# Two fused blocks on one core: the recurrent gates run among the other projections, the convolution's inputs are multiplied on their way out of the banks, and two output chunks are opened in free score banks

## What is computed

```python
u = rms_norm(h, mix_norm[l])
q, k, v, sc_b, sc_c, sc_x, lru_x, lru_g = jnp.split(u @ w_in[l], IN_SPLIT_POINTS, axis=-1)
y_da = diff_attention(q, k, v, ...)                   # 4 heads, two softmaxes each, then a norm per head
y_sc = sc_b * causal_dwconv(sc_c * sc_x, sc_conv_w[l])          # width 256
xr = causal_dwconv(lru_x, lru_conv_w[l]) + lru_conv_b[l]        # width 256
y_lru = jax.nn.gelu(lru_g) * rg_lru(xr, lru_wa[l], ...)         # two gates, then a scan over the tokens
h = h + jnp.concatenate([y_da, y_sc, y_lru], axis=-1) @ w_out[l]
x = h + 0.5 * swiglu(rms_norm(h, ffn2_norm[l]), ...)
```

## Time and profile before

| what | value |
|---|---|
| median of 3 runs | 3335.58 us |
| the profiled execution, its own time | 3334.97 us |
| its span, first to last instruction | 3333.0 us |
| TensorE busy | 3183.0 us, 96% |
| VectorE busy | 1540.9 us, 46% |
| ScalarE busy | 716.5 us, 21% |
| GpSimd busy | 1975.6 us, 59% |
| mean granted TensorE clock | 0.979 |

### The profile page before, as it was taken

The page is one execution under the profiler, slowest core; times in us unless marked ns, Lnnn a source line. Parts: engine busy times, 40 slices in busy tenths (PEclk is TensorE's granted clock), DMA queues, the critical chain, the costliest instruction groups (busy, mean ns, idle before and its releaser), DMA issues.

```text
span 3333.0 us, 44944 instructions
## 1 busy us (share of the span) xinstructions
PE 3183.0 (96%) x15410; PEld 2618.1 (79%) x15410; DVE 1540.9 (46%) x1978; ACT 716.5 (21%) x1454; POOL 1975.6 (59%) x1566
## 2 busy tenths in 40 slices
PE   8998999989989999699998989999999997999998
PEld 7777888877778888588887678888888886788886
DVE  6577322275772322644227564431444247564422
ACT  3353110044531100411112221110111012321110
POOL 6324766653237666377666357776677665277763
PEclk9999999999999999899999999999999998999999
DMA  4111322221113222122222112223222232122221
GB/s 168 52 39 51 107 97 98 95 90 51 39 51 107 94 95 98 54 94 94 101 98 101 58 64 94 95 95 101 91 99 94 97 109 83 39 89 99 96 95 64
DMA packets 82023, 286.47 MB, mean 86 GB/s; under 512 B 9531, under 2 KB 13020, under 8 KB 81628
## 3 DMA queue, kind: packets, MB, share of 16 engines
q1 hardware_dynamic: 76032, 275.81, 24.6%
q10 hardware_dynamic: 5852, 8.78, 0.8%
HBM read 280.89 MB, written 3.67 MB: 85 GB/s over the span
## 4 chain that ended last, share of the span: by engine, by line
PE 89%; DVE 6%; issue 2%; ACT 1%; POOL 1%; DMA 0%; DVEq 0%; SPq 0%; ACTq 0%; POOLq 0%
PE bank_v L452 19%; PE bank_v L454 18%; PE bank_v L453 18%; PE bank_a L452 8%; PE bank_a L453 8%; PE bank_a L454 8%; PE bank_v L667 1%; PE bank_a L646 1%; PE bank_s L800 1%; PE bank_v L815 1%; PE bank_s L685 1%; DVE mix L1948 1%; PE bank_a L491 0%; DVE lru_x L1931 0%; PE bank_s L803 0%
## 5 line engine op out<-in xcount | busy, mean ns | idle before, releaser
L426 POOL TENSOR_TENSOR w_lo<-raw,w_hi 128x1024 fp32r<-128x1024 f32 x520 | 1321.4, 2541 | 41.6
L423 POOL TENSOR_TENSOR zero<-zero 128x1 f32<-128x1 f32 x520 | 132.3, 255 | 1280.0 <-PE bank_v L454 967.0
L452 PE MATMUL bank_v<-xn_hi,w_hi 128*128 128x512 f32 (+1 forms) x1648 | 633.9, 385 | 41.2 <-DVE da_v L2001 31.7
L453 PE MATMUL bank_v<-xn_lo,w_hi 128*128 128x512 f32 (+1 forms) x1648 | 624.5, 379 | 0.0
L454 PE MATMUL bank_v<-xn_hi,w_lo 128*128 128x512 f32 (+1 forms) x1648 | 624.4, 379 | 0.0
L424 POOL CAST w_hi<-raw 128x1024 fp32r<-128x1024 f32 x520 | 556.5, 1070 | 0.0
L452 PE MATMUL bank_a<-xn_hi,w_hi 128*128 128x512 f32 (+1 forms) x1264 | 485.9, 384 | 40.1 <-DVE xn_lo L1461 21.5
L453 PE MATMUL bank_a<-xn_lo,w_hi 128*128 128x512 f32 (+1 forms) x1264 | 480.9, 380 | 0.0
L454 PE MATMUL bank_a<-xn_hi,w_lo 128*128 128x512 f32 (+1 forms) x1264 | 480.7, 380 | 0.0
L452 PE MATMUL bank_v<-h_hi,w_hi 128*128 128x512 f32 (+1 forms) x1100 | 419.7, 382 | 0.0
L454 PE MATMUL bank_v<-h_hi,w_lo 128*128 128x512 f32 (+1 forms) x1100 | 418.6, 381 | 0.0
(11 more groups left out here) (342 smaller groups left out, 3374.5 us busy)
## 6 DMA issues: line engine op xcount, KB each, us to landing
raw<-in_w_stream SPq DMA_DIRECT2D x520, 512.0 KB, 3.3
rope<-in_rope ACTq DMA_DIRECT2D x2, 1024.0 KB, 4.9
da_v<-t_rows ACTq DMA_DIRECT2D x2, 1024.0 KB, 5.6
out<-resid SPq DMA_DIRECT2D x4, 512.0 KB, 2.6
t_rows<-t_row ACTq DMA_DIRECT2D x1, 1536.0 KB, 5.7
resid<-in_x SPq DMA_DIRECT2D x4, 256.0 KB, 4.2
resid<-in_x ACTq DMA_DIRECT2D x4, 256.0 KB, 9.4
mla_v<-in_alibi ACTq DMA_DIRECT2D x2, 512.0 KB, 5.9
```

Source lines behind the costliest of these rows:

```text
L423: pool.tensor_tensor(zero[:, 1:2], zero[:, 0:1], zero[:, 0:1], ALU.add)
L426: pool.tensor_tensor(w_lo[:, u, :], raw[:, u, :], w_hi[:, u, :].bitcast(F32), ALU.subtract).then_inc(*w_split.done(("unit", u)))
L452: pe.matmul(out, lhs_hi, rhs_hi, start=first, stop=False)
L453: pe.matmul(out, lhs_hi, rhs_lo, start=False, stop=False)
```

## The change

On TensorE the small `lam_sums` matmul moves ahead of `lx`, `scc` 0 moves into a DVE bank and stands ahead of the gate matmuls, and `scc` 1 and both `scx` stand behind them. ACT no longer copies `scc`. On DVE the convolution `xr` of half 0 starts after `lx` 0 alone; a new instruction makes the square of the factor; `keep_scc` multiplies `scc` by it out of its bank, and `keep_scx` multiplies `scx` by that out of its bank, in place of three instructions for each half. The evictions of `q2` 0 and `k2` 0 move behind the recurrence product of half 0 and of half 1. At the end of `diff()` the first two `wout` chunks open in the two score banks of item 14 and take chunks 6 and 7 at once, the third takes a DVE bank; the two row banks are those of item 15; `head_values(3)`, the row matmuls, the sums and DVE's evictions and low parts are reordered around them.

```diff
 OPEN_ENDS = 3
-EARLY_CHUNKS = ((6, 7), (4, 5))
+EARLY_CHUNKS = (6, 7, 4, 5)
...
+        end_read = signal("end_read")
...
+
+        def row_bank(h):
+            return bank_s[s_read.slot(("diff", 3, TT - 1, h % 2), 4)]
+
+        def early_end_bank(c):
+            return bank_s[s_read.slot(("diff", 3, TT - 2, c), 4)]
+
+        def end_kept(c):
+            return (end_read if c < 2 else v_read).after(("wout", c))
...
                 def open_end(c):
                     unit(("wout", c))
-                    banks[c] = stat_bank if c == 2 else v_bank(("wout", c))
+                    if c < 2:
+                        pe.wait_ge(*s_read.after(("diff", 3, TT - 2, 1)))
+                    banks[c] = early_end_bank(c) if c < 2 else v_bank(("wout", c))
...
                 def head_row(h):
                     pe.wait_ge(*diag_ready.after(("headrow", h)))
-                    if h == 3:
-                        pe.wait_ge(*value.after(("subln", 0)))
-                    pe.matmul(bank_s[h % 3][:, :], ones[:, :], diag[:, h * TT:(h + 1) * TT, :], start=True, stop=True
+                    if h >= 2:
+                        pe.wait_ge(*value.after(("subln", h - 2)))
+                    pe.matmul(row_bank(h)[:, :], ones[:, :], diag[:, h * TT:(h + 1) * TT, :], start=True, stop=True
                               ).then_inc(*sums.done(("headrow", h)))
...
                     filler(n)
-                    if DIFF_LAG <= n < len(heads) + DIFF_LAG:
+                    if n >= DIFF_LAG:
                         m = n - DIFF_LAG
                         turn(("diff", *heads[m]), probs2[:, m % 4 * 2, :], heads[m][1] + 1)
+                    if n in (8, 12):
+                        head_sums(n // 4 - 2)
                     if n == len(heads):
-                        open_end(0)
-                    if n in (len(heads), len(heads) + 1):
-                        end_chunks(0, EARLY_CHUNKS[n - len(heads)])
-                    h = n // 4 - 2
-                    if n % 4 == 0 and h >= 0:
-                        early_sums(("subln", h), squared.after(("subln", h)), work[:, h, :])
...
-                for h in range(3):
-                    if h == 0:
-                        pe.wait_ge(*s_read.after(("diff", 3, TT - 1, 1)))
-                    head_row(h)
-                open_end(1)
-                end_chunks(1, EARLY_CHUNKS[0] + EARLY_CHUNKS[1])
-                early_sums(("subln", 3), squared.after(("subln", 3)), work[:, 3, :])
+                        for c in range(2):
+                            open_end(c)
+                            end_chunks(c, (6, 7))
+                head_sums(2)
+                for k in (4, 5):
+                    for c in range(2):
+                        end_chunks(c, (k,))
+                head_values(3)
+                pe.wait_ge(*s_read.after(("diff", 3, TT - 1, 1)))
+                head_row(0)
+                head_row(1)
+                open_end(2)
+                end_chunks(2, EARLY_CHUNKS)
+                head_row(2)
+                head_sums(3)
                 end_chunks(0, range(3))
                 end_chunks(1, range(3))
                 head_row(3)
-                open_end(2)
-                end_chunks(2, EARLY_CHUNKS[0] + EARLY_CHUNKS[1] + (0, 1, 2))
+                end_chunks(2, range(3))
                 for c in range(OPEN_ENDS):
                     end_chunks(c, (3,)).then_inc(*w_used.done(("wout", c)))
...
                 spread("rms2")
+                pe.wait_ge(*dve_step.after("lam_products"))
+                pe.matmul(stat_bank[:, 8:10], ones[0:HD, :], small[0:HD, 64:66], start=True, stop=True,
+                          skip_group_check=True).then_inc(*sums.done("lam_sums"))
                 for n in range(2):
                     project(("lx", n), v_bank)
-                for n in range(2):
-                    project(("scc", n), a_bank)
-                for n in range(2):
-                    project(("scx", n), v_bank)
-                pe.wait_ge(*dve_step.after("lam_products"))
-                pe.matmul(stat_bank[:, 0:2], ones[0:HD, :], small[0:HD, 64:66], start=True, stop=True
-                          ).then_inc(*sums.done("lam_sums"))
+                project(("scc", 0), v_bank)
                 for c in range(2):
                     pe.wait_ge(*lru_in.after("lru_w"))
                     pe.wait_ge(*dve_step.after(("xr", c)))
@@ -976,6 +991,9 @@
                         b = a_bank(("gate", name, c))
                         pe.matmul(b[:, :], lru_w[:, 2 * m + c, :], xr[:, c, :], start=True, stop=True
                                   ).then_inc(*sums.done(("gate", name, c)))
+                project(("scc", 1), v_bank)
+                for n in range(2):
+                    project(("scx", n), v_bank)
                 project(("q2", 0), v_bank)
                 project(("k2", 0), v_bank)
                 project_rows("v2", 4, S)
...
                     copy_bank(("lg", n), w_used, lru_g[:, n, :])
                 for n in range(2):
-                    copy_bank(("scc", n), w_used, sc_c[:, n, :])
-                for n in range(2):
                     act.wait_ge(*value.after(("lg", n)))
...
                         late_hi(1)
+                        subln_square(2)
                     if n >= DIFF_LAG:
                         keep_turned(n - DIFF_LAG)
                     if n == 14:
                         late_hi(0)
-                    if head_ending_at(n - DIFF_LAG - 2) is not None:
-                        subln_square(head_ending_at(n - DIFF_LAG - 2))
-                    h = n // 4 - 2
-                    if n % 4 == 0 and h >= 0:
-                        keep_sums(("subln", h), h)
-                    if n == len(heads):
-                        head_root(0, 3)
+                    if n in (7, 11):
+                        subln_square((n - 7) // 4)
+                    if n in (8, 12):
+                        keep_sums(("subln", n // 4 - 2), n // 4 - 2)
+                keep_sums(("subln", 2), 2)
+                head_root(0, 3)
...
                 factor("rms2")
                 for n in range(2):
                     times_factor(lru_g[:, n, :], value.done(("lg", n)), a_read.after(("lg", n)))
-                for n in range(2):
-                    times_factor(lru_x[:, n, :], v_read.done(("lx", n)), w_used.after(("lx", n)), v_bank(("lx", n))[:, :])
-                dve.wait_ge(*v_read.after(("lx", 1)))
+                step(dve.tensor_tensor(factor_squared[:, 0, :], scale_by[:, :], scale_by[:, :], ALU.mult), "factor_squared")
+
+                def keep_scc(n):
+                    dve.wait_ge(*w_used.after(("scc", n)))
+                    dve.tensor_tensor(sc_c[:, n, :], v_bank(("scc", n))[:, :], factor_squared[:, 0, :], ALU.mult
+                                      ).then_inc(*v_read.done(("scc", n)))
+
+                def keep_scx(n):
+                    dve.wait_ge(*w_used.after(("scx", n)))
+                    dve.wait_ge(*v_read.after(("scc", n)))
+                    dve.tensor_tensor(sc_x[:, n, :], v_bank(("scx", n))[:, :], sc_c[:, n, :], ALU.mult
+                                      ).then_inc(*v_read.done(("scx", n)))
+
                 for c in range(2):
+                    times_factor(lru_x[:, c, :], v_read.done(("lx", c)), w_used.after(("lx", c)), v_bank(("lx", c))[:, :])
+                    dve.wait_ge(*v_read.after(("lx", c)))
                     w = lambda k: par2[:, C2["lru_w"] + 2 * k + c:C2["lru_w"] + 2 * k + c + 1]
                     step(dve.tensor_scalar(xr[:, c, :], lru_x[:, c, :], w(3), col(par2, C2, "lru_b", c),
                                            ALU.mult, ALU.add), ("lconv", c, 0))
@@ -1888,13 +1916,7 @@
                         ins = dve.scalar_tensor_tensor(out=xr[:, c, d:S], in0=lru_x[:, c, 0:S - d], scalar=w(3 - d),
                                                        in1=xr[:, c, d:S], op0=ALU.mult, op1=ALU.add)
                         step(ins, ("lconv", c, d) if d < 3 else ("xr", c))
-                for n in range(2):
-                    key = ("scx", n)
-                    times_factor(sc_c[:, n, :], dve_step.done(("scc", n)), a_read.after(("scc", n)))
-                    times_factor(sc_x[:, n, :], v_read.done(key), w_used.after(key), v_bank(key)[:, :])
-                    dve.wait_ge(*dve_step.after(("scc", n)))
-                    dve.wait_ge(*v_read.after(key))
-                    step(dve.tensor_tensor(sc_x[:, n, :], sc_c[:, n, :], sc_x[:, n, :], ALU.mult), ("sc", n))
+                keep_scc(0)
...
+                keep_scc(1)
...
                 for c in range(2):
                     dve.wait_ge(*act_step.after(("tanh", c)))
-                    (keep_k if c else keep_q)(0)
                     step(dve.tensor_scalar(lru_x[:, c, :], gate_r[:, c, :], 1.0, None, ALU.add), ("t1", c))
                     step(dve.reciprocal(lru_x[:, c, :], lru_x[:, c, :]), ("t2", c))
```

(41 more changed lines are left out.)

14 lines of the change are left out of this document (8 added, 6 removed).

## The result

The changed kernel took 3295.92 us (median of 4 runs, 3294.91 to 3301.32); the kernel before, on the same chip, 3337.5 us (4 runs, 3335.48 to 3342.0). The ratio is 0.9877, 95% interval 0.986 to 0.9894.

What follows compares the result with a forecast made beforehand. TensorE, 89% of the chain that ended last, was taken as the bound. Gains of 23.6 - 1.0 + 9.2 + 7.5 = 39.3 us off 3335.0 gave 3295.7, 3296.3 on the median's scale, stated as 3297 us; range 3283 to 3317.

Steps and rivals of the forecast that it cites:

- `k2` 0 ends at 1801.5: On TensorE ahead of `v2`: the same matmuls reordered, so `k2` 0 ends at 1801.5 where it ended at 1801.9.
- The queue behind `scx` 1: On DVE: both recurrence chains and two evictions take 16.1 us, bounds 10.2 and 18.0, so `v2` waits 6.0 us.
- Clock behind the wait: Behind the wait ahead of `v2`: TensorE at 1.2 GHz costs 1.7 us, from 1.4 to 2.0.
- Front: Up to the end of `q2` 1: the 15.8 us wait goes, gain 11.8 us per layer, bounds 9.6 and 18.9.
- The cover that I gave 1 us: Ahead of `v2` tile 1's eviction: DVE's table, convolution and low parts end 1 us before `v2` tile 1.
- The items: In the items: GpSimd's splits stretch DVE's scaling of weights, mostly hidden; charged 0.5 us per layer, bounds 0 and 3.
- The end: End of `diff()`: TensorE's waste falls to 2.2 us; gain 9.2 us in the first layer, 7.5 in the second.
- the signs that I had named: `q2` 1 unwaited; `v2` wait 4 to 8 us; `scx` evictions 0.69 us; weights' waits 1 to 2 us; tail PEclk 1.00.
- In phase with GpSimd: Rival, chance 0.15: DVE is first at most meetings with GpSimd, `v2` waits under 2.5 us; 3282 to 3287 us.
- Short waits cost clock: Rival, chance 0.17: short waits in the tail or stretched weights in the items cost clock or time; 3305 to 3318 us.
- The clock stays down: Rival, chance 0.04: after the 6 us wait TensorE stays at 1.2 GHz through `v2` and `q2` 1; 3348 us.
- The wait only moves: Rival, chance 0.04: the two chains hold `v2` as long as `v2` tile 1 held `q2` 1; 3318 to 3335 us.

Runs made afterwards that it cites:

- e3: The changed kernel with `k2` 0's eviction moved ahead of the scan of the second half's chain on DVE; 3287.7 us, ratio 0.9851.
- e1: The kernel before with only the change's projection and gate part, the end of `diff()` as before; 3312.62 us, ratio 0.9923.
- e11: The changed kernel with 15 useless matmuls (3.4 us) on TensorE between `k2` 0 and `v2`; 3291.33 us, ratio 0.9856.
- e7: The changed kernel with two more DVE reciprocals, 6.7 us, behind `k2` 0's eviction and ahead of the table's low part; 3297.36 us, ratio 0.987.

## Why the prediction was right, step by step

**`k2` 0 ends at 1801.5.** It ended at 1807.00, which on the clock of before (5.52 us earlier) is 1801.5.

**The queue behind `scx` 1, 16.1 us.** It took 13.1 us (1797.23 to 1810.34), so `v2` waited 3.5 us and not 6.0. The mis-sized term is this queue. I charged both scans at 2.10 and more, taking 2.10 for a scan's short length; the changed kernel shows 1.22 us, so the 2.10 of the earlier trace rows was itself stretched (GpSimd's cast had started 0.02 us ahead of it). That is 1.8 of the 3.0 us. The rest comes of fewer stretched instructions: the first `L1959` took 0.77 us, ahead of GpSimd's subtraction by 0.3 us. A count was wrong too, without effect on the sum: DVE loses six full-width instructions per layer and gains five, so one fewer and not three (1976 in all against 1978).

The Trainium skill (SBUF — State Buffer, section "Who interferes with whom") says that whichever engine holds the ports first keeps them for its whole instruction. By that rule a scan that starts first should lengthen GpSimd's instruction; the trace agrees, 1.99 in place of 1.04 us at 1807.21.

**Clock behind the wait, 1.7 us.** `v2` to the first score is 28.0 us without half clock (e3, both layers) and was 30.6 and 29.5 us here: 2.6 and 1.5 us. My bounds, 1.4 to 2.0, were too narrow above.

**Front, 11.8 us per layer.** 13.1: the wait was 2.5 us shorter, and in the first layer the clock took 0.9 us of that back; the last 0.3 us is that `v2` to the first score takes 28.0 us at 2.4 GHz, where I added 22.3 and 5.4. In the second layer the clock behind the wait took 0.2 us less than forecast, and the stretch behind ffn2's sums, which stands in no term of mine, took 1.5 us; 0.4 us of that layer I did not follow. (By the same sum my upper bound is 1848.7 - 1829.3 = 19.4 us per layer, not 18.9.) The cover that I gave 1 us was 8.6 us, for a reason that I had not seen: TensorE's wait keeps GpSimd idle for 7 us, and the convolution runs there at short lengths. In e3, where the wait is 1 us and GpSimd busy, nothing of the cover is left: DVE takes 17.7 us for the table and the convolution in place of 13.7, and begins tile 1's eviction, 0.74 us long, without idle time ahead of it; `q2` 1 starts just behind its end, at 1823.76 us.

```profile
1822.97 0.74 DVE L2030 TENSOR_SCALAR da_v<-bank_v,small 128x512 f32<-128x512 f32 x1
```

**The items, -0.5 us per layer.** 0.0: 73.83 us before, 73.83 and 73.84 after. GpSimd's splits there are hidden.

**The end, 9.2 and 7.5 us.** 9.0 and 6.0. The waits were 0.93 and 0.61 us where I had 1.5 and 0.7: DVE's scaling took 0.49 us and the instruction behind it 2.76, where before they took 2.12 and 0.75. The first layer gained no more than forecast even so: 0.3 us went into the longer wait at ffn2's sums, and 0.6 us I did not follow. In the second layer the waits were followed by 3.4 us at 1.2 GHz, worth 1.6 us.

**Behind it.** I charged nothing there, and 2.2 us were lost. The wait at the second layer's ffn2 sums grew from 1.07 to 1.35 us, and 1.2 GHz followed it, which the profiled run of before did not show at that place. It is the stretch that costs, and the wait's length does not decide it: e1 had the stretch behind a wait of 1.06 us (375.0 us to the end), e11 had none behind 1.35 us (372.6 us, against 372.8 before). The same 4.16 us behind these sums in the changed kernel and in e11:

```profile
2924.52:2928.68 4.16, 4.16 (x16) 3.48 (x17) 2.69 (x6) 1.98 (x3) 3.34 (x2) 0.63 0.39 126
...
2916.84:2921.00 4.16, 4.16 (x22) 3.62 (x23) 2.73 (x6) 1.98 (x3) 3.38 (x3) 1.00 0.41 126
```

Sum: 26.3 + 0.0 + 15.0 - 2.2 = 39.1 by the rounded stretches, against 23.6 - 1.0 + 16.7 = 39.3. The four terms were off by +2.7, +1.0, -1.7 and -2.2 us and cancelled. The mechanism was right, that `k2` 0's eviction becomes the wait and `v2` tile 1 is covered; that the sum came within 0.3 us is luck.

Of the signs that I had named, `q2` 1 followed `v2` without a wait, and the evictions of `scx` took 0.69 us. The wait ahead of `v2` was below its 4 to 8 us, the weights' wait below its 1 to 2 us, and at the second layer's end of `diff()` PEclk was not 1.00 throughout.

**The rivals.** In phase with GpSimd: in the queue DVE was first at two of six meetings (1797.15 and 1807.14), and the wait of 3.5 us lies between 2.5 and 6.0. Short waits cost clock: true in mechanism, at 1.6 us in one layer here and 3.1 us in e3, short of the 3 to 7 us per layer that would have made it the result. The clock stays down: against it, every stretch at 1.2 GHz behind `v2`'s wait ended within 5.9 us of the restart. The wait only moves: it moved, and shrank from 15.8 to 3.5 us.

What stays open: why the short waits (0.6 to 1.4 us) in the tail and at ffn2's sums lower the clock in some layers and executions of the same list and not in others. The runs show that taking the waits away takes the stretch away, and not what decides where they remain.

## What to carry to other kernels

Move the long serial chain's inputs forward until the next consumer's own work covers it, and then ask what the new queue puts behind it: here the new order alone gave half of the front gain, and the cheaper evictions gave the other half only because the new order put them on the way to a bank. Don't count an engine's idle time as free cover when another engine, which starts working as soon as the wait is gone, stretches its instructions. Several waits of 1 us are worth removing for the clock behind them as much as for themselves, but each move uncovers the next wait, which must be looked for first.

## What the runs showed of the hardware

- A DVE scan of 128x512 takes 1.22 us alone, and 2.10 and 3.29 us beside GpSimd.
- A DVE instruction of one SBUF input can be stretched too: `L1972` takes 0.47 us, and took 2.61 us behind GpSimd's subtraction in e7 (row below).

```profile
1824.48 2.61 DVE L1972 TENSOR_SCALAR mix<-mix_hi_late,par 128x512 f32<-128x512 f32 x1
```

- A DVE multiplication that takes one input from a bank kept its 0.69 us in all these rows, with GpSimd busy or not.
- Behind waits of 3.5 to 8.5 us TensorE's stretch at 1.2 GHz ended 3.2 to 5.9 us after the restart, whatever the wait's length; 3.4 us of useless matmuls in the wait's place kept PEclk at 1.00.
